# A mixture-of-experts stage entered another way: first expert's tokens gathered by 0/1 products, its pass written out ahead of the loop, the router with its weights stationary, norms in two halves

## What is computed

```python
def rmsnorm(x, g):
    y = xf * lax.rsqrt(jnp.mean(xf * xf, axis=-1, keepdims=True) + EPS)
...
h = rmsnorm(x, norm_ffn[i]) * (1 + sc2) + sh2
...
def moe_ffn(h, w_router, w1, w2):                 # 8 experts, D_FF = 3584
    logits = (t @ w_router).astype(jnp.float32)
    top_v, top_i = lax.top_k(logits, TOP_K)       # TOP_K = 2
    probs = jax.nn.softmax(top_v, axis=-1)
    ...
    for e in range(N_EXPERTS):
        out = out + combine[:, e:e + 1] * swiglu(t, w1[e], w2[e])
```

## Time and profile before

| | us |
|---|---|
| median of 3 runs | 1906.11 |
| lowest, highest | 1902.64, 1907.49 |
| the profiled execution's own time | 1906.12 |
| its span, first to last instruction | 1904.4 |
| PE busy in the span | 1801.2 |
| from the end of the second convolution product to the first expert product | 752.8 to 800.1 |
| the nine passes | 800.1 to 1875.7 |

### The profile page before, as it was taken

How to read it: one execution, slowest core, us unless ns; L and a number is a source line. 1 busy time by engine, 2 the same in 40 slices (tenths; PEclk the granted TensorE clock), 3 DMA queues, 4 the chain that set the end, 5 groups by cost and what they waited for, 6 DMA issues and landing times.

```text
span 1904.4 us, 24867 instructions
## 1 busy us (share of the span) xinstructions
PE 1801.2 (95%) x8964; PEld 1484.9 (78%) x8964; DVE 1416.2 (74%) x1568; ACT 1070.5 (56%) x1067; POOL 48.1 (3%) x95
## 2 busy tenths in 40 slices
PE   6999999799999998599999999999999999999993
PEld 3778876799997875488888888888888888888883
DVE  1544435565655783499999999999999999999995
ACT  1222224433343222377777777777777777777772
POOL 0001100000000000100000000000000000000001
PEclk8999999899999999599999999999999999999997
DMA  9466678354545653399999999999999999999972
GB/s 391 159 250 230 220 260 320 126 197 172 196 174 207 261 210 132 110 381 379 381 377 376 377 380 381 376 381 374 379 381 378 378 380 377 377 377 372 384 297 88
DMA packets 63002, 568.57 MB, mean 299 GB/s; under 512 B 7268, under 2 KB 7396, under 8 KB 15204
## 3 DMA queue, kind: packets, MB, share of 16 engines
q1 hardware_dynamic: 54144, 539.13, 73.3%
q0 software_dynamic: 5392, 19.41, 2.8%
q10 hardware_dynamic: 3412, 9.28, 1.2%
HBM read 549.43 MB, written 18.36 MB: 298 GB/s over the span
## 4 chain that ended last, share of the span: by engine, by line
PE 88%; DVE 4%; DMA 3%; issue 2%; ACT 2%; POOL 0%; DVEq 0%; POOLq 0%; SPq 0%; ACTq 0%
PE ps L1531 22%; PE ps L1533 22%; PE ps L1532 22%; PE ps L1396 6%; PE ps L1623 3%; PE ps L1393 3%; DMA ring<-mix 2%; PE ps L1318 2%; PE ps L1524 1%; PE ps L1613 1%; PE ps L1707 1%; DVE w_lo L1279 1%; ACT w_hi L840 1%; PE ps L1449 1%; PE ps L1419 1%
## 5 line engine op out<-in xcount | busy, mean ns | idle before, releaser
L1279 DVE TENSOR_TENSOR w_lo<-ring,w_hi 128x1536 fp32r<-128x1536 f32 x504 | 873.8, 1756 | 76.4 <-ACT w_hi L840 76.0
L840 ACT ACTIVATE w_hi<-ring 128x1536 fp32r<-128x1536 f32 x504 | 751.0, 1492 | 232.3 <-PE ps L1533 221.9
L1531 PE MATMUL ps<-w_hi,hg 128*128 128x512 f32 x1072 | 424.8, 396 | 6.7 <-DVE w_lo L1279 4.4
L1532 PE MATMUL ps<-w_lo,hg 128*128 128x512 f32 x1072 | 419.5, 391 | 0.0
L1533 PE MATMUL ps<-w_hi,hg 128*128 128x512 f32 x1008 | 393.6, 390 | 0.0
L1533 PE MATMUL ps<-w_hi,hid 128*128 128x512 f32 x680 | 265.8, 391 | 0.0
L1531 PE MATMUL ps<-w_hi,hid 128*128 128x512 f32 x616 | 241.9, 393 | 3.1 <-DVE hid L1273 3.1
L1532 PE MATMUL ps<-w_lo,hid 128*128 128x512 f32 x616 | 240.0, 390 | 0.0
L1531 PEld LDWEIGHTS ps<-w_hi,hg 128*128 128x128 f32 x1072 | 202.5, 189 | 47.6 <-DVE w_lo L1279 4.8
L1532 PEld LDWEIGHTS ps<-w_lo,hg 128*128 128x128 f32 x1072 | 202.8, 189 | 40.8
L1533 PEld LDWEIGHTS ps<-w_hi,hg 128*128 128x128 f32 x1008 | 189.7, 188 | 40.2
(11 more groups left out here) (235 smaller groups left out, 1670.9 us busy)
## 6 DMA issues: line engine op xcount, KB each, us to landing
ring<-moe SPq DMA_DIRECT2D x252, 1536.0 KB, 8.3
ring<-mix SPq DMA_DIRECT2D x92, 1024.0 KB, 6.9
ring<-ff SPq DMA_DIRECT2D x28, 1536.0 KB, 6.5
xg<-work POOLq DMA_DIRECT2D x12, 512.0 KB, 6.5
so<-xg POOLq DMA_DIRECT2D x10, 512.0 KB, 8.8
yg<-so ACTq DMA_DIRECT2D x10, 512.0 KB, 9.2
work<-c POOLq DMA_DIRECT2D x8, 257.0 KB, 7.1
c_out<-work ACTq DMA_DIRECT2D x8, 257.0 KB, 6.0
```

Of the source, the lines that this page charges most:

```text
L840: act.activation(w_hi[:, s % W_BUFS, :], ring[:, sl, s % 2 * CUT * ROW:(s % 2 + 1) * CUT * ROW], ACT.Copy).then_inc(hi_ready, 1)
L1279: TT(w_lo[:, s % W_BUFS, :], ring[:, slot(ST_MOE + s // 2), s % 2 * CUT * ROW:(s % 2 + 1) * CUT * ROW], w_hi[:, s % W_BUFS, :].bitcast(f32 ...
L1531: pe.matmul(out, a_hi, b_hi, start=start, stop=False)
L1532: pe.matmul(out, a_hi, b_lo, start=False, stop=False)
```

## The change

Five edits go together. (1) **Norms in halves**: the residual is multiplied and added group by group, with `x0_ready` for group 0; ACT's square waits for that alone, and POOL takes each group's root by itself. Of the eight pieces of group 1, DVE takes four and ACT the other four (`hT2_ready`) after its own eight. (2) **Router**: the 8 columns of weights are stationary and 256 tokens move; the 8 by 256 result is copied by DVE and turned by two transposes. PE turns the tokens back in two parts around these. ACT does all four copies to `htok`. (3) **First gather**: DVE compares each token's row within expert 0 with a row of numbers, and makes a 128 by 128 matrix of 0 and 1 for each group (`first_hot`); PE multiplies `htok` with it (16 products), which gives the turned tokens of the first pass without DRAM. (4) **First pass** outside the loop, which now begins at 1. Its first two cuts are rounded and subtracted earlier, within the router's operations (`expert_high`, `expert_low`). (5) The plan and the weights of the two experts are worked out by DVE within the first pass, at its fifth cut (`plan_items`).

```diff
             def norm_root(q):
-                pool.wait_ge(ss_ready, q + 1)
-                pool.wait_ge(ss1_ready, q + 1)
-                pool.tensor_scalar(mean[:, :], ss[:, :], EPS, None, ALU.add).then_inc(mean_ready, 1)
-                roots[0] += 1
-                pool.wait_ge(mean_ready, roots[0])
-                pool.tensor_tensor(rstd[:, :], mean[:, :], half[:, :], ALU.pow).then_inc(rstd_ready, 1)
+                for g in range(G):
+                    c = slice(g, g + 1)
+                    pool.wait_ge([ss_ready, ss1_ready][g], q + 1)
+                    pool.tensor_scalar(mean[:, c], ss[:, c], EPS, None, ALU.add).then_inc(mean_ready, 1)
+                    roots[0] += 1
+                    pool.wait_ge(mean_ready, roots[0])
+                    pool.tensor_tensor(rstd[:, c], mean[:, c], half[:, c], ALU.pow
+                                       ).then_inc([rstd_ready, rstd1_ready][g], 1)
...
-                act.wait_ge(x_ready, q + 1)
+                if q == 0:
+                    act.wait_ge(x_in_s, 16)
+                else:
+                    act.wait_ge(x0_ready, q)
...
+                act.wait_ge(turned, 4 * q + 4)
+                for i in range(4):
+                    k = 4 + i
+                    act.activation(hT[:, k, P:T], ps[:, YB + 3, i * P:(i + 1) * P], ACT.Identity,
+                                   scale=scl[:, q, k, 1:2], bias=mod[:, 3 * q, k, 1:2]).then_inc(hT2_ready, 1)
...
             gate_copies(3)
+            def expert_high(i, s):
+
+                sl = slot(ST_MOE + s // 2)
+                if s % 2 == 0:
+                    act.wait_ge(loaded[sl], i * (16 * FC // SLOTS) + 16 * ((ST_MOE + s // 2) // SLOTS + 1))
+
+                act.wait_ge(stage_used, i * CUTS + (ST_MOE + s - W_BUFS + 1))
+                act.activation(w_hi[:, s % W_BUFS, :], ring[:, sl, s % 2 * CUT * ROW:(s % 2 + 1) * CUT * ROW],
+                               ACT.Copy).then_inc(hi_ready, 1)
+
+            for n in range(FIRST_CUTS):
+                expert_high(0, n)
+            for g in range(G):
+                for b in range(2):
+                    act.wait_ge(htok_psum, 2 * g + b + 1)
+                    act.activation(htok[:, g, b * 512:(b + 1) * 512], ps[:, 2 * g + b, :], ACT.Copy
+                                   ).then_inc([htok_ready0, htok_ready1][g], 1)
             act.wait_ge(route_gap, 1)
             act.activation(tk[:, 3, :], tk[:, 2, :], ACT.Exp).then_inc(route_exp, 1)
-            for b in range(2):
-                act.wait_ge(htok_psum, b + 1)
-                act.activation(htok[:, 0, b * 512:(b + 1) * 512], ps[:, YB + b, :], ACT.Copy).then_inc(htok_ready0, 1)
 
             def hg_high(i):
 
...
-                for b in range(4):
-                    ins = STT(gv[:, b, :], gv[:, b, :], scale, ps[:, YB + b, :], ALU.mult, ALU.mult)
-                link(ins)
-                TT(x[:, :, :], x[:, :, :], gate, ALU.add).then_inc(x_ready, 1)
+                for g in range(G):
+                    for b in range(2 * g, 2 * g + 2):
+                        ins = STT(gv[:, b, :], gv[:, b, :], scale, ps[:, YB + b, :], ALU.mult, ALU.mult)
+                    link(ins)
+                    TT(x[:, g, :], x[:, g, :], gate[:, g, :], ALU.add).then_inc([x0_ready, x_ready][g], 1)
...
+            dve.wait_ge(route_raw, 1)
+            dve.tensor_copy(lg_turned[0:EXPERTS, :], ps[0:EXPERTS, YB, 0:T]).then_inc(route_copied, 1)
+
+            def expert_low(i, s):
+
+                dve.wait_ge(hi_ready, i * CUTS + (FF_CUTS + s + 1))
+                TT(w_lo[:, s % W_BUFS, :], ring[:, slot(ST_MOE + s // 2), s % 2 * CUT * ROW:(s % 2 + 1) * CUT * ROW],
+                   w_hi[:, s % W_BUFS, :].bitcast(f32), ALU.subtract).then_inc(split_ready, 1)
+
             dve.wait_ge(route_psum, 1)
...
+            expert_low(0, 0)
             dve.wait_ge(pos_psum, 1)
+            link(dve.tensor_copy(at_pos, ps[:, COUNTS, 0:G * EXPERTS].rearrange("p (g e) -> p g e", g=G)))
+            for g in range(G):
+                ins = TS(first_hot[:, g, :], iota, at_pos[:, g, 0:1], sel[:, g, 0:1], ALU.is_equal, ALU.mult)
+            ins.then_inc(hot_ready, 1)
+            expert_low(0, 1)
...
+            def plan_items():
+
+                dve.wait_ge(route_exp, 1)
...
+                    if begun and s == W_BUFS:
+                        plan_items()
+                        start[0] = n_chain[0]
...
-            pe.wait_ge(gateb_ready, 14)
-            for g in range(G):
-                for k in range(KD):
-                    ins = pe.matmul(ps[:, MISC, g * EXPERTS:(g + 1) * EXPERTS], tokens(hT, k, g), wr[:, k, :],
-                                    start=(k == 0), stop=(k == KD - 1))
-            ins.then_inc(route_psum, 1)
+            for k in range(KD):
+                ins = pe.matmul(ps[0:EXPERTS, YB, 0:T], wr[:, k, :], hT[:, k, :], start=(k == 0), stop=(k == KD - 1))
+            ins.then_inc(route_raw, 1)
             pe.wait_ge(gateb_ready, 16)
 
-            for g in range(G):
+            def tokens_back(g):
+
                 for b in range(2):
                     for i in range(4):
-                        ins = pe.transpose(ps[:, YB + 2 * g + b, i * P:(i + 1) * P], tokens(hT, 4 * b + i, g), ident)
+                        ins = pe.transpose(ps[:, 2 * g + b, i * P:(i + 1) * P], tokens(hT, 4 * b + i, g), ident)
                     ins.then_inc(htok_psum, 1)
+
+            tokens_back(0)
+            pe.wait_ge(route_copied, 1)
+            for g in range(G):
+                ins = pe.transpose(ps[:, LOGITS, g * EXPERTS:(g + 1) * EXPERTS], lg_turned[0:EXPERTS, g * P:(g + 1) * P],
+                                   ident[0:EXPERTS, 0:EXPERTS])
+            ins.then_inc(route_psum, 1)
+            tokens_back(1)
...
+            def first_gather():
+
+                pe.wait_ge(htok_ready0, 2)
+                pe.wait_ge(htok_ready1, 2)
+                pe.wait_ge(hot_ready, 1)
+                for k in range(KD):
+                    for g in range(G):
+                        ins = pe.matmul(ps[:, UB + k // 4, (k % 4) * P:(k % 4 + 1) * P], htok[:, g, k * P:(k + 1) * P],
+                                        first_hot[:, g, :], start=(g == 0), stop=(g == G - 1))
+                ins.then_inc(gathered, 1)
...
-            gather(0)
-            pe.wait_ge(plan_ready, 1)
-            items = pe.value_load(plan[0:1, 0:1], min_val=EXPERTS, max_val=ITEMS)
-            with pe.Fori(0, items) as i:
+            first_gather()
...
+            expert(0)
+            pe.wait_ge(plan_ready, 1)
+            items = pe.value_load(plan[0:1, 0:1], min_val=EXPERTS, max_val=ITEMS)
+            with pe.Fori(1, items) as i:
+                expert(i)
```

More of the change, by code:

```diff
@@ L816, in _, with expert @@
             hg_high(0)
-            act.wait_ge(plan_ready, 1)
-            items = act.value_load(plan[0:1, 0:1], min_val=EXPERTS, max_val=ITEMS)
-            with act.Fori(0, items) as i:
+            def expert(i, begun):
                 for s in range(CUTS + 1):
```

118 lines of the change are left out of this document (60 added, 58 removed).

## The result

| | before | changed |
|---|---|---|
| median, us | 1907.26 (1902.64 to 1907.88, 6 runs) | 1895.77 (1891.26 to 1897.64, 6 runs) |
| ratio | | 0.9942 [0.9928, 0.9956] |
| profiled execution's own time | 1906.12 | 1891.26 |

The account below looks back on a forecast made before the run. TensorE, busy 1801 of 1904 us, bounds the kernel, with a chain of waits before the experts to shorten. Gains 15.5 + 1.1 + 1.2 - 0.8 = 17.0 us off 1906.12 give 1889.1 us, range 1882.5 to 1895.5.

Parts of the forecast that it names:

- the term for the norms in halves: Norms 1, 2 and 3: adding and scaling group 0 early gains 1.2, loses 0.8 and gains 2.3 us; 2.7 together.
- from squares to turned tokens nothing changes for that group: Norm halves: group 0, added 2.35 us earlier, keeps its old times from squares through root and scaling to turned tokens.
- Norm 1: Norm ahead of the dense part: the halves gain 1.2 us, with 0.9 and 1.4 as bounds.
- Norm 2, 0.8 lost: Norm ahead of the convolution mixer: ACT's four more pieces make PE start at 618.9 instead of 618.08, 0.8 us lost.
- First expert product, 15.5 us: End of the chain from norm 3 through router and gather: first expert product at 784.6 instead of 800.07, 15.5 us earlier.
- Router 5.7: New router: eight products, five at the slow clock and three at the fast, 5.7 us instead of 6.97.
- rival A: Clock stays at 2.4 GHz throughout: router 3.6, gather 3.7, first expert product about 780.4, total 1883.7 us; chance 0.15.
- Gather 5.5: First gather by 16 products on PE: 5.5 us, the middle between 3.73 at 2.4 GHz and 7.5 at 1.2.
- rival B: Clock stays at 1.2 GHz through router and gather: first expert product 788.0, total 1891.3 to 1893.6 us; chance 0.17.
- Early subtraction 0.6: Ahead of the 0/1 tiles: a weights' subtraction moved early on DVE delays copy and comparisons, costing 0.6 us.
- Clock at the start of the pass 1.1: First expert products: dense gather beforehand saves half of the 2.3 us that the slow clock cost before, 1.1 us.
- Handover, DVE in the first pass, code, stores: 0: First pass and entry to the loop: register load, DVE's plan, straight-line code and stores beside the pass booked at zero.

Follow-up runs that it names:

- e17: Kernel before with only the norms in two halves; gather through DRAM, passes in the loop, eight-column router: ratio 1.0011 to the kernel before.
- e3: Changed kernel in which DVE, in norms 1 and 3, waits for POOL's root of group 0 before adding group 1: 1893.88 us, 0.9921 to the kernel before.
- the second trace: The changed kernel run and traced again with nothing edited: 1895.07 us median.
- e6: Changed kernel with the first pass's tokens fetched through DRAM again, 0/1 tiles made but unused: 1909.33 us, 1.0001 to the kernel before.
- e16: Kernel before with only the 0/1 gather; all passes in the loop, no early cuts, norms whole, eight-column router: 0.9943 to the kernel before.
- e8: Changed kernel with norms whole and the eight-column router as before, keeping 0/1 gather, outside pass and early cuts: 1893.47 us, 0.9918 to the kernel before.
- e5: Changed kernel with the old router, eight columns moving, without the copy and two small turns: 1893.8 us, 0.9931 to the kernel before.
- e15: Kernel before with only the first expert's pass moved outside the loop: 0.9988 to the kernel before.
- e18: Changed kernel with DVE waiting for POOL's root in norms 1 and 3 and twenty filler products, three in norm 2: 1884.31 us, 0.9874 to the kernel before.
- e1: Changed kernel with the norms whole again, both groups' root at once: 1895.07 us, 0.9934 to the kernel before.
- e12: Changed kernel with norms whole, eight-column router as before, and seven filler products around the gather: 1894.47 us, 0.993 to the kernel before.

## Why the prediction was wrong

The step that failed is the term for the norms in halves, 2.7 us (2.3 + 1.2 - 0.8). It rests on "from squares to turned tokens nothing changes for that group", which is false, and it ends at norm 2's first product, behind which the sum has nothing. Alone the halves gained nothing: 1.0011 [0.9995, 1.0027], 2 us lost with 1 gained and 5 lost as bounds (e17). The difference to the forecast's 2.7, 4.8 us with 3 to each side, covers most of the 5.5 us by which the forecast missed. Against its own steps:

- **"From squares to turned tokens nothing changes for that group".** POOL's root for group 0 takes 2.9 us (755.46 to 758.33) instead of 0.9 to 1.0, because DVE works beside it (e3 shows the cause). So group 0 is scaled and turned 0.55 us earlier and not 2.35, and the router starts 0.6 us earlier and not 2.3 (13.52 and 13.46 us behind the residual's start in the two traces, 14.08 before). Norm 1: 1.2 forecast, between 0.7 lost and 0.1 lost in the changed kernel's traces (257.7, 257.1 against 257.0). Beside this row the Trainium skill (SBUF — State Buffer, Who interferes with whom) says that VectorE and GpSimd share a pair of SBUF ports as an exclusive lock, and that a VectorE instruction with two inputs in SBUF contends with a GpSimd instruction that reads SBUF. The trace agrees: gate addition and squares each have two SBUF inputs, each started first (by 0.04 and 0.13 us), and POOL's instructions end 0.07 and 0.42 us behind them.
- **Norm 2, 0.8 lost:** 1.0 in the second trace, 1.6 in the first, whose turn took 3.32 at the lower clock. The size was right but for the clock. Behind it lay a cost that the sum put at nothing: 1.7 us at 1.2 GHz in the convolution's first products (136.5 against 134.8), in the second trace and in most of the variants, but not in the first trace.
- **First expert product, 15.5 us.** 12.9 in the first trace, 15.0 in the second. Gather through PE instead of DRAM: right, and shown to carry nearly the whole gain (e6 gives all of it back, e16 alone has 10.7). That the second trace comes within 0.5 is luck: the 1.7 us that the halves did not bring were made good by a router 2.1 us shorter than booked.
- **Router 5.7:** 5.30 and 3.61. In the first trace the clock rose on the way, as forecast (granted 0.69, 0.50 and 0.96 in the windows of 2 us from 765 on); in the second it was at 2.4 GHz throughout, as in rival A. The prediction's own "five products at 0.9 and three at 0.45" add up to 5.85. The 3.6 beside it is the price at 2.4 GHz from the first product on, which the rule quoted there, with the throttled clock as the default, doesn't give by itself. That the new form gains by raising the clock is not shown: the old form took 5.41 and 5.61 in e8 and e5 and 5.33 in e17, and 6.96 or 6.97 in six other traces, and TensorE's instructions in e8 up to there are those of e16, which had 6.97.
- **Gather 5.5:** 6.57 and 6.01. The term was mis-sized by 1.1 and 0.5; the clock was at its lower level for most of it, which is half of rival B.
- **Early subtraction 0.6:** `at_pos` waited from 775.8 to 776.1 for it in the first trace, and not at all in the second: 0.3 and 0. **Rounding and subtraction 2.4:** the tokens' subtraction ends 2.3 us behind the gather. Right.
- **Clock at the start of the pass 1.1:** 0.8 and 0.9 (1106.05 to 1105.3 and 1105.2). Right.
- **Handover, DVE in the first pass, code, stores: 0.** Right (e15; the first pass is busy for 118.67 us).

For the second trace, near the median, the misses are 0.5 (norm 3 to first product) + 1.3 (norm 1) + 0.2 (norm 2) + 1.7 (behind it) + 0.2 (pass) = 3.9, so 13.1 of 17.0; the first column differs by 1.7 from the mean of the three traces of before (348.2), which gives the 11.3 between its 1895.72 and their mean of 1907.0. Pairs on one chip gave ratios of 0.9942 and 0.9925, 11 to 14 us.

**Open:** why the clock falls at norm 2 in all traces with the 0/1 gather or the halves but e18, and in none of the four with neither. For the halves the longer idle time is a candidate. For the gather with whole norms (e1, e8, e12, e16) there is none: its code does not run there, and up to there e16's and e8's instructions are those of before. In e1 and e12 TensorE had waited longer than before for a load of `mix` ahead of the turn (2.12 and 2.34 us against 1.42), in e8 and e16 it had not (1.44 and 1.43), so that is not the whole of it, and few traces are not enough to exclude chance. That the time lost is the clock's is shown (e18), what triggers the fall is not.

## What to carry to other kernels

When a norm or softmax is cut in halves so that one half's small GpSimd step lies beside VectorE's work on the other, price that step as if it waited for each VectorE instruction with two SBUF inputs, or give VectorE a wait there. Count also what the halves do to TensorE's idle time: here it grew by 1 us in norm 2, and behind it the products ran at the lower clock until filler products were put in. Where TensorE idles for a few microseconds ahead of dense work, price its first products at the lower clock, and try products whose result nobody uses in the idle time; place them only where the engine waits in every run. Replacing a trip through DRAM by 0/1 products on the idle TensorE brought nearly all that this change gained.

## What the runs showed of the hardware

- A GpSimd operation on 128 numbers takes 0.22 or 1.26 us, its root 0.57 or 1.52, by what VectorE does meanwhile.
- The router's 8 products with 256 moving columns took 3.61, 5.08, 5.30, 6.11, 6.33 or 6.52 us by the clock alone (16 products with eight columns moving: 5.33, 5.41, 5.61, or 6.96 and 6.97); filler ahead of it in norm 3 did not settle it (6.52, 6.52, 5.08).
- The same kernel reaches norm 1 at 343.9 or 349.9 us, by where the granted clock is low on the way; its two traces differ by 4.5 us in all.
- Twenty products that compute nothing make the kernel about 10 us faster than the same change without them on the same chip (ratios 0.9874 [0.9851, 0.9896] and 0.9925 [0.9905, 0.9944]), e3's wait included.
